# Moving one input projection of a hybrid encoder layer ahead of the first pass's output stages

## What is computed

```python
h = rmsnorm(x, norm_mix_g);  u = h @ w_in                 # the combined input projection
y_a = rglru_mixer(...); y_b = ssd_mixer(...)              # four sequence mixers, each with a
y_c = gdn_mixer(...);   y_d = s5_mixer(...)               # state that runs over the tokens
x = x + concat(y_a, y_b, y_c, y_d) @ w_out
x = x + cross_attend(rmsnorm(x, norm_cross_g), mem_k, mem_v, w_cq, w_co)   # 256 memory tokens
x = x + swiglu(rmsnorm(x, norm_ffn_g), w_gate, w_up, w_down)               # hidden width 2816
y = rmsnorm(x, norm_final_g)
# before it: mem_k, mem_v = rmsnorm(mem, norm_mem_g) @ w_ck, @ w_cv
```

## Time and profile before

| | |
|---|---|
| Runs | 4091.99 us median, 4088.88 to 4100.78 |
| Profiled execution | 4092.89 us, its span 4091.1 us |
| TensorE matmul busy | 3659.4 us, 89% |
| VectorE busy | 2256.5 us, 55% |
| ScalarE busy | 1335.2 us, 33% |
| GpSimd busy | 126.5 us, 3% |
| Mean granted TensorE clock | 0.942 of full speed |

### The profile page before, as it was taken

How to read it: one execution, slowest core, us unless ns; L and a number is a source line. 1 busy time by engine, 2 the same in 40 slices (tenths; PEclk the granted TensorE clock), 3 DMA queues, 4 the chain that set the end, 5 groups by cost and what they waited for, 6 DMA issues and landing times.

```text
span 4091.1 us, 63447 instructions
## 1 busy us (share of the span) xinstructions
PE 3659.4 (89%) x24122; PEld 3547.7 (87%) x24122; DVE 2256.5 (55%) x4638; ACT 1335.2 (33%) x2474; POOL 126.5 (3%) x354
## 2 busy tenths in 40 slices
PE   6777868889798999998899998899998899999998
PEld 5766768889788999988899998899997899998998
DVE  6656744377674766573645573555564556553323
ACT  5443332254533333432322332323232322322101
POOL 2400000000000000000000000000000000000000
PEclk8977977799898999999999999999999999999999
DMA  6654476577767677768566668456667556567776
GB/s 216 228 180 155 164 237 224 168 237 269 250 221 276 232 251 265 269 209 281 180 210 208 231 218 282 171 189 226 222 226 255 191 188 210 198 210 253 248 252 218
DMA packets 371566, 912.03 MB, mean 223 GB/s; under 512 B 34752, under 2 KB 174528, under 8 KB 370752
## 3 DMA queue, kind: packets, MB, share of 16 engines
q1 hardware_dynamic: 371264, 907.99, 64.3%
HBM read 733.28 MB, written 174.57 MB: 222 GB/s over the span
## 4 chain that ended last, share of the span: by engine, by line
PE 50%; issue 20%; DVE 13%; DMA 5%; ACT 4%; DVEq 3%; POOLq 2%; SPq 1%; POOL 1%; ACTq 1%; PEld 0%; PEldq 0%
PE banks L461 14%; PE banks L463 13%; PE banks L462 13%; DMA wlo_sb<-kept_dram 2%; DVE wlo_sb L1121 2%; DVE uc_sb L1212 2%; PE banks L1611 1%; PE banks L1605 1%; DVE m_p_sb L2178 1%; PE banks L877 1%; PE banks L1614 1%; DMA kept_dram<-wlo_sb 1%; ACT whi_sb L929 1%; DMA ldb_sb<-y_dram 1%; DVE m_p_sb L2148 1%
## 5 line engine op out<-in xcount | busy, mean ns | idle before, releaser
L461 PE MATMUL banks<-hh_sb,whi_sb 128*128 128x384 f32 (+1 forms) x3360 | 1153.1, 343 | 117.2 <-DMA wlo_sb<-kept_dram 27.4
L462 PE MATMUL banks<-hh_sb,wlo_sb 128*128 128x384 f32 (+1 forms) x3360 | 1122.3, 334 | 0.0
L463 PE MATMUL banks<-hl_sb,whi_sb 128*128 128x384 f32 (+1 forms) x3360 | 1121.2, 334 | 0.0
L461 PEld LDWEIGHTS banks<-hh_sb,whi_sb 128*128 128x128 f32 x3360 | 652.7, 194 | 145.4 <-issue 46.4
L462 PEld LDWEIGHTS banks<-hh_sb,wlo_sb 128*128 128x128 f32 x3360 | 653.7, 195 | 1.4 <-issue 0.3
L463 PEld LDWEIGHTS banks<-hl_sb,whi_sb 128*128 128x128 f32 x3360 | 652.0, 194 | 0.0
L461 PE MATMUL banks<-g_hi_sb,whi_sb 128*128 128x384 f32 (+2 forms) x1504 | 514.5, 342 | 73.2 <-DVE x_sb L1317 26.8
L463 PE MATMUL banks<-g_lo_sb,whi_sb 128*128 128x384 f32 (+2 forms) x1504 | 501.3, 333 | 0.0
L462 PE MATMUL banks<-g_hi_sb,wlo_sb 128*128 128x384 f32 (+2 forms) x1504 | 501.2, 333 | 0.0
L461 PEld LDWEIGHTS banks<-g_hi_sb,whi_sb 128*128 128x128 f32 x1504 | 295.5, 196 | 87.5 <-DVE x_sb L1317 30.1
L1317 DVE TENSOR_TENSOR x_sb<-x_sb,banks 128x384 f32<-128x384 f32 (+2 forms) x400 | 202.4, 515 | 281.1 <-PE banks L463 272.1
(11 more groups left out here) (433 smaller groups left out, 5235.2 us busy)
## 6 DMA issues: line engine op xcount, KB each, us to landing
whi_sb<-kept_dram SPq DMA_DIRECT2D x504, 512.0 KB, 3.8
wlo_sb<-kept_dram SPq DMA_DIRECT2D x504, 512.0 KB, 4.9
raw_sb<-w SPq DMA_DIRECT2D x176, 512.0 KB, 5.3
kept_dram<-whi_sb SPq DMA_DIRECT2D x112, 512.0 KB, 5.5
kept_dram<-wlo_sb SPq DMA_DIRECT2D x112, 512.0 KB, 6.4
uc_dram<-uc_sb SPq DMA_DIRECT2D x90, 192.0 KB, 2.8
ldb_sb<-x_t SPq DMA_DIRECT2D x72, 192.0 KB, 4.7
plain_sb<-w SPq DMA_DIRECT2D x32, 256.0 KB, 4.8
```

The lines of the kernel that those rows point to most:

```text
L461: eng.matmul(out, xh, yh, start=first, stop=False)
L462: eng.matmul(out, xl, yh, start=False, stop=False)
L463: return eng.matmul(out, xh, yl, start=False, stop=last)
```

## The change

Only the order and what hangs on it are edited. The last four memory sections (`fv` of heads 2 and 3) and A(2) are now put behind A(1), ahead of B(0); the preps of A(2) ride on those four sections. The window of mixer 0 ends with A(2) in place of A(1). The window of mixer 1 is B(0) alone, and ends six dense sections before the end of B(0). The preps of y for pass 1 and the squares of the final norm of pass 0 ride on the last four `d` sections of B(0), `st` and `final` of pass 0 follow it directly, and x of pass 1 is loaded at the first `w` of B(1). From B(1) on the order is as before. Two waits are adapted: the buffer of the softmax is shared with the projection's output tiles, so pass 0 waits for the stores of A(2), and the sample caches wait for A(2)'s last use of the h buffer.

```diff
-    h, n = new_h("A", 1), new_norm("A", 1)
-    spread(kv[-4:], preps("A", 1, h, n))
-    secs += kv + stage_a(1, h, n)
+
+    for p, part in ((1, kv[:-4]), (2, kv[-4:])):
+        h, n = new_h("A", p), new_norm("A", p)
+        spread(part[-4:], preps("A", p, h, n))
+        secs += part + stage_a(p, h, n)
     windows.append((0, first - 2, len(secs) - 2))
     for p in range(NP):
         hy = new_h("Y", p)
-        if p < NP - 1:
+        if secs[-1].kind == "z":
             spread(secs[-1:], preps("Y", p, hy))
         else:
             spread([s for s in secs if s.kind == "d"][-4:], preps("Y", p, hy))
...
-        if p + 2 < NP:
+        if 0 < p < NP - 2:
             h, n = new_h("A", p + 2), new_norm("A", p + 2)
...
-            windows.append((p + 1, first, len(secs) - (2 if p + 2 < NP else 11)))
+            windows.append((p + 1, first, len(secs) - (2 if secs[-1].kind == "z" else 11)))
...
-                end = Q_END[min(s.p + 1, NP - 1)]
+                end = Q_END[min(max(s.p + 1, 2), NP - 1)]
...
-            if s.p >= 2 and (s.kind == "u" and s.b >= 16 or s.kind == "z"):
+            if s.p >= 3 and (s.kind == "u" and s.b >= 16 or s.kind == "z"):
                 sp_x(eng, s.p - 1, s.b - 16 if s.kind == "u" else 2 + s.a)
             elif s.kind == "w" and s.a == 0:
-                for q in range(KD // 2 if s.p in (0, NP - 1) else 0):
+                for q in range(KD // 2 if s.p in (0, 1, NP - 1) else 0):
                     sp_x(eng, s.p, q)
...
-                eng.wait_ge(full, H_FILLS[HS.index(("A", 1))])
+                eng.wait_ge(full, H_FILLS[HS.index(("A", 2))])
```

## The result

| | before | changed |
|---|---|---|
| Runs beside each other | 4096.39 us median (4 runs, 4088.88 to 4100.96) | 4047.47 us median (4 runs, 4038.55 to 4054.13) |
| Profiled execution | 4092.89 us | 4053.16 us, span 4051.4 |
| TensorE busy | 3659.4 us | 3642.1 us |
| Mean granted clock | 0.942 | 0.947 |

The ratio is 0.9884 [0.987, 0.9898]: faster by 1.2%, 49 us between the medians, 40 between the two profiled executions. The forecast was 4068 in a range of 4030 to 4106. The direction was right and the time is in the range, but twice the forecast gain came.

A forecast was written before the change was run, and what follows sets the result against it. TensorE, busy 89%, was taken to set the time, with gains in the first 1100 us. Memory rest, A(1) and A(2) -62, B(0) +29, handoffs +9 gave -24 us: 4068 us forecast, range 4030 to 4106.

The forecast's parts named there:

- Nothing moves: Rival: A(1)'s excess is the sample chunk's own chain, a section costs 1.9 us anywhere; 4094 us, chance 0.17.
- A(1), -41 forecast: In A(1), 11 mixer sections leave at 3.7 us each, saving 41 us.
- price (d): Mixer section cost from A(1) with handoff, 229 us and 34 sections, against A(3), 141 and 10: 3.7 us each.
- the bound of 138 us for A(1): A(1)'s time if all above dense work and 1.9 us per mixer section went.
- Memory rest, -26 forecast: Rest of the memory stage: 7 mixer sections leave, saving 26 us, including the 11.6 us wait at L1846.
- 7 x 3.7: Memory rest: seven mixer sections leaving, each priced at 3.7 us, 26 us in all.
- A(2), +12 - 7 forecast: A(2): 5 more mixer sections at 2.5 us cost 12 us; 7 of the 10 us start gap are won.
- B(0), +29 forecast: B(0): 5 more mixer sections in attention cost 15 us, 8 more in feed-forward 14 us; bounds 8 and 48.
- The handoffs, +9 forecast: Handoff into B(0) unchanged; into B(1) the gap grows from 7 to 15.5 us, so +9, bounds 0 and +20.
- Both bounds of B(0) with half of the bounds of part 1: Rule for the range: B(0) growth of 8 to 48 us, half the memory rest and A(1) bounds (34 to 124).
- The clock comes back: Rival: more mixer work lifts the clock in B(0)'s attention, up to 49 us; 4043 us at half, chance 0.12.
- B(0) has no room: Rival: B(0)'s 3 us dense sections are too short; at 5.5 us per section it grows 72, 4111 us, chance 0.15.

The follow-up runs named there:

- the dense one: The changed kernel with mixer 0's 50 sections dealt only to the eight memory sections (12) and A(1) (38): 4090.28 us, ratio 0.999 to the kernel before.
- the old order's twins: Kernel before, mixer 1 in B(0) alone, A(2)'s kind-Q preps removed from B(0): 4107.98 us; same with mixer 1's window ending six dense sections earlier: 4080.64 us.
- the order alone: Changed kernel with mixer 0 only on the eight memory sections and A(1), mixer 1 starting at A(2): 4108.69 us, ratio 1.0036 to the kernel before.

## Why the prediction was right in direction and short in size

**The mechanism.** Crowding was the cause, as forecast: in the new order, thinning mixer 0 is worth 33 us (4090.28 against 4057.23, on the same chip), against a density a little above that of the kernel before (38 sections in A(1), not 34); the waits of mixer steps in A(1) go 46, 16, 50 us over the kernel before, the changed one and the dense one; and the order without the thinning wins nothing. "Nothing moves", which had a mixer section cost its bare work anywhere, falls by the stages A: 6 to 7 us each between 24 and 34 sections, not 1.9.

**The deal.** The planner puts 5 sections on the eight memory sections and 24 in A(1), not 6 and 23. So 8 left the memory rest and 10 left A(1); the sum of the two terms, 18 x 3.7, stays.

**A(1), -41 forecast, -67 measured.** The term was mis-sized. The 3.7 us of price (d) is a mean over 24 sections from 10 to 34, and the change takes off the top of them. Between first `u` and last `z` the ten that left were worth 71 us, 7.1 each, where a section costs some 2 us up to 18 of them. The rows before could have bounded it: a stage A's bare work, 94 us by the price per column, was known, and the bound of 138 us for A(1) is what it nearly came to, 142. The sign "A(1) in 155 to 180 us" was missed on the good side.

**Memory rest, -26 forecast, +7 measured.** The step that failed is "7 x 3.7". The wait at L1846 did go, 11.6 to 0.4, as the test had it, though not for the reason given: a later start alone leaves it at 10.2. But cutting the stage in two gave it a second end with preps of its own, and there they meet the mixer: 58 us for four sections. The forecast counted the preps' DMAs and squares and not what they do to the three mixer sections beside them; with the mixer kept off, the piece takes 34, though the other stages of the window then pay nearly all of it back. The two misses, 33 us dear and 26 cheap, cancel; the forecast for the two together was 7 us too good. That is luck.

**A(2), +12 - 7 forecast.** Between first `u` and last `z` it took 113.1 us with 18 sections against 110.8 with 13, only +2.3. It had stood above its fair price before: without a mixer the same stage took 87.2 us in the old order (where mixer 1 was in B(0) alone) and 77.1 in the new. So five sections more cost about 10 us, and what left the stage (the final norm of pass 0 with its squares, the writing of its results, the loads of x) gave about as much back; no run has these one by one. The forecast had priced the squares at 0 and had no term for the rest. The 14.6 us of its start are now inside the memory piece, where they cost what was just said.

**B(0), +29 forecast, +14 and +7 measured in two profiles.** Both parts were priced too dear. Eight sections more in the feed-forward cost 6 us by the windows (307 to 313), against 14 forecast; in two kernels of the old order that differ in this window alone (38 and 46 sections) it is 0.9 us each. The attention took 251 us before and 259 and 251 after, against 15 forecast; there the deal decides, for 20 to 21 sections gave between 251 and 277 us. The changed kernel was dealt a good hand. With the other deal, by the old order's twins, it would have given back an estimated 22 us of its 49. The sign "B(0) from first `w` to last `d` 575 to 605 us" was missed too, with 569 and 562.

**The handoffs, +9 forecast.** Right. By the forecast's own measure, from the last `d` to the third `w` less three `w`, the gap is 31.0 - 12.5 = 18.5 us (1187.22 to 1218.23), against 7 before: +11.5. Up to the eighth `w` it is +10 (56.7 us from the last `d`, against 55.6 from the last `z` before, 8.8 of them the second `z`). The wait for x is that of the earlier trace rows.

**The range.** "Both bounds of B(0) with half of the bounds of part 1" gives 4068 - 21 - 28 = 4019 at its lower end, not 4030. The measured 4047 lies in either.

**"The clock comes back".** Rejected in the size: 0.73 and 0.75 in the attention of B(0), and 0.74 and 0.81 in the second profile, against 0.69 and 0.74, not above 0.85 and nothing like the 0.94 of B(1). The Trainium skill (TensorE: Matmul & The Clock Gate, Part 1: The HAM clock gate), cited there for activity lifting the clock, is not contradicted in its direction by these rows, and hardly borne out: the whole attention had a mean of 0.71 with no mixer section, 0.71 and 0.73 in two kernels with 16, and 0.73 to 0.78 with 17 to 21, while two profiles of one kernel gave 0.74 and 0.78.

**"B(0) has no room".** Not at 46 sections, but at 67 in the feed-forward, where the gain is gone: there a section costs 3.0 to 3.5 us.

## What to carry to other kernels

When a chain of small dependent steps is woven into dense work, its price per step is not constant. Here it was 2 us up to about one step per dense section and 6 to 7 between 1.3 and 2; with narrower dense sections it rose to 3 by the time each carried one. So deal no denser than about one, and take the price of steps that leave from the crowded end, not from a mean over the whole stage. A count does not price a weave: the same 67 steps, dealt to slightly other places, cost 22 us more, so try a few deals before judging the edit that needs them. Look at the ends of a stage first, since preparations for the next stage use the same engines as the woven chain. And before calling a kernel "the order alone", count what the planner deals where: here the shorter window had made it denser.

## What was not expected of the hardware

In the sample tokens' attention a stretch with 24 more matmuls took 19 us less (138 against 157) and TensorE was busy for 8 us less, at a granted clock of 0.80 in place of 0.76: fewer waits and the higher clock came together. But the changed kernel's two profiles differ in the same way with nothing changed, 118.82 us busy at 0.75 and 110.66 at 0.81, so the mean clock of one stretch in one profile is a weak measure of an edit. And two profiled executions of the changed kernel differ by 9 us in the later 2800 us, so the first 1300 us of a trace tell more about an edit there than the whole span.
